# Scores of the forgetting attention: two heads on two row tiles, split operands, and a new order of the second block

## The reference, cut to what matters

```
log_f = log_sigmoid(fl + b_forget)            # (L, 12)
F = cumsum(log_f)                             # forget sums, one row of 512 per head
s = (q * 64**-0.5) @ k.T + F[t] - F[s]        # causal: s <= t, else -1e30
p = softmax(s);  o = p @ v
y_fox = o * silu(gf)
```

## Time and profile before

| | |
|---|---|
| median of 3 runs | 1972.76 us (1971.41 to 1973.77) |
| span of the profiled execution | 1970.0 us |
| PE busy | 1925.6 us (98%) |
| DVE, ACT, POOL busy | 1198.0, 923.5, 945.3 us |
| chain that ended last, share of PE | 89% |

### The profile page before, as it was taken

One profiled execution on the slowest core, in us unless ns is written; L12 is line 12 of the kernel. 1 busy time (PEld: TensorE's weight loads), 2 busy tenths in 40 slices (PEclk: granted clock), 3 DMA queues, 4 the chain that ended last, 5 costly groups with the idle time before them and its releaser, 6 DMA issues.

```text
span 1970.0 us, 28999 instructions
## 1 busy us (share of the span) xinstructions
PE 1925.6 (98%) x11395; PEld 1595.0 (81%) x11395; DVE 1198.0 (61%) x1932; ACT 923.5 (47%) x1747; POOL 945.3 (48%) x702
## 2 busy tenths in 40 slices
PE   6999999999999999999999999999999999999998
PEld 5878787888788878888888888888688777889986
DVE  6587979694566646664544440345765575876664
ACT  4555756564455544233434342344655454534442
POOL 1343323234534226564444444454474561788883
PEclk9999999999999999999999999999999999999999
DMA  8256353543321117664332334335122323233333
GB/s 310 76 168 191 110 182 117 182 145 105 107 62 55 43 56 285 226 227 158 96 107 86 107 85 148 99 115 187 55 74 81 82 55 115 85 98 97 89 121 138
DMA packets 92327, 242.48 MB, mean 123 GB/s; under 512 B 28192, under 2 KB 31392, under 8 KB 90784
## 3 DMA queue, kind: packets, MB, share of 16 engines
q1 hardware_dynamic: 89312, 232.24, 37.3%
q10 hardware_dynamic: 2880, 8.39, 1.1%
HBM read 223.14 MB, written 14.29 MB: 121 GB/s over the span
## 4 chain that ended last, share of the span: by engine, by line
PE 89%; DVE 3%; POOL 3%; ACT 2%; DMA 1%; issue 1%; SPq 0%; ACTq 0%; DVEq 0%
PE ps L1002 21%; PE ps L1003 20%; PE ps L1013 20%; PE ps L1372 3%; PE ps L1447 2%; PE ps L1434 2%; PE ps L1038 1%; PE ps L1037 1%; PE ps L1422 1%; PE ps L1349 1%; PE ps L1048 1%; PE ps L1509 1%; PE ps L1103 1%; PE ps L1110 1%; PE ps L1104 1%; POOL wlo L3069 1%
## 5 line engine op out<-in xcount | busy, mean ns | idle before, releaser
L3068 POOL TENSOR_TENSOR wlo<-raww,whi 128x512 fp32r<-128x512 f32 x217 | 303.6, 1399 | 668.3 <-ACT whi L1576 667.8
L1576 ACT CAST whi<-raww 128x1024 fp32r<-128x1024 f32 (+2 forms) x299 | 295.4, 995 | 197.3 <-PE ps L1013 134.4
L3069 POOL TENSOR_TENSOR wlo<-raww,whi 128x512 fp32r<-128x512 f32 x217 | 309.7, 1427 | 0.0
L1002 PE MATMUL ps<-hT_h,whi 128*128 128x512 f32 (+1 forms) x688 | 251.3, 374 | 2.4 <-DVE st L2480 1.7
L1003 PE MATMUL ps<-hT_l,whi 128*128 128x512 f32 (+1 forms) x688 | 244.6, 365 | 0.0
L1013 PE MATMUL ps<-hT_h,wlo 128*128 128x512 f32 (+1 forms) x688 | 152.4, 364 | 0.0
L1002 PEld LDWEIGHTS ps<-hT_h,whi 128*128 128x128 f32 x688 | 129.8, 189 | 27.3 <-issue 3.4
L1003 PEld LDWEIGHTS ps<-hT_l,whi 128*128 128x128 f32 x688 | 129.9, 189 | 21.9 <-issue 1.7
L1013 PEld LDWEIGHTS ps<-hT_h,wlo 128*128 128x128 f32 x688 | 119.2, 189 | 20.7 <-issue 0.5
L1002 PE MATMUL ps<-h_h,whi 128*128 128x512 f32 x336 | 130.7, 389 | 0.0
L1003 PE MATMUL ps<-h_l,whi 128*128 128x512 f32 x336 | 130.7, 389 | 0.0
(11 more groups left out here) (642 smaller groups left out, 4863.8 us busy)
## 6 DMA issues: line engine op xcount, KB each, us to landing
ec<-csd SPq DMA_DIRECT2D x32, 1024.0 KB, 8.2
raww<-in_w_up SPq DMA_DIRECT2D x44, 512.0 KB, 3.6
modr<-in_w_mod SPq DMA_DIRECT2D x32, 512.0 KB, 5.9
raww<-in_w_xbc SPq DMA_DIRECT2D x24, 512.0 KB, 3.8
raww<-in_w_gl SPq DMA_DIRECT2D x24, 512.0 KB, 3.9
raww<-in_w_z SPq DMA_DIRECT2D x16, 512.0 KB, 3.6
raww<-in_w_g SPq DMA_DIRECT2D x16, 512.0 KB, 3.6
raww<-in_w_os SPq DMA_DIRECT2D x16, 512.0 KB, 4.0
```

Of the source, the lines that this page charges most:

```text
L1002: e.matmul(o, whi[:, i, c], hi(k)[:, t0:t1], start=(k == 0), stop=False)
L1576: e.copy(o, x.rearrange("p (k c) -> p k c", c=64) if p == plan.first["dt", 0] else x).then_inc(*w_high.mark(("high", p)))
L3068: e.tensor_tensor(o[:, 0:512], x[:, 0:512], h[:, 0:512].bitcast(F32), ALU.subtract).then_inc(*p_wlow.mark(("first half", p)))
L3069: e.tensor_tensor(o[:, 512:1024], x[:, 512:1024], h[:, 512:1024].bitcast(F32), ALU.subtract).then_inc(*p_wlow.mark(("split", p), ("raw fre ...
```

## The change: what it does

1. q and k of two heads stay together, head 2p in rows 0 to 63 and head 2p+1 in rows 64 to 127, as a high part (ACT, one instruction of 128 rows) and a low part (DVE, one scalar_tensor_tensor out of PSUM) in the tiles fhead0 and fhead1. The bank of `fq` is marked "out of" by the DVE instruction, no longer by ACT.
2. The step `fscore` is now for a pair p and a group g of query rows: g 0 is rows 0 and 1, g 1 row 2, g 2 row 3. For each row it issues three fp32r products (high by high, low by high, high by low), head by head in turn on rows 0 to 63 and 64 to 127 of the array and into two banks; then one fp32r product that picks the head's row of forget sums; then two bf16 products for the mask (128 and 64 columns).
3. The forget sums are split in a high and a low row set in the tile frows by DVE, which also builds the pick matrix, two identities and two masks in bf16. FT, its 12 DMAs and the clearing of qk on POOL are gone; POOL clears eyes and frows.
4. DVE and ACT do softmax work for both heads of a pair within one step.
5. The order of the second block is one written list, `second_block_steps()`. Eight `fpt` of a pair are grouped (`turns(p)`), and `fqout 0` stands behind `s5bar 1`.

```diff
+def second_block_steps():
...
+    o = [("fq", 0), ("s5zero",)] + [("s5u", m) for m in range(3)]
+    o += [("s5bar", 0), ("fq", 6), ("s5bar", 1), ("fqout", 0), ("fqout", 6)]
+    o += [tm(0, 0)] + pw(0, 1) + [tmout(0, 0), tm(0, 1)] + pw(1, 3) + [tmout(0, 1), tm(0, 2)] + pw(3, 4)
+    o += [tmout(0, 2), tm(0, 3)] + pw(4, 6) + [tmout(0, 3), ("fq", 1)] + pw(6, 8) + [("fqout", 1)]
+    o += [("fscore", 0, 0)] + pw(8, 9) + [("fscore", 0, 1)] + pw(9, 10) + [("fscore", 0, 2)] + pw(10, 11)
+    o += [("fq", 7), ("fscored", 0)] + pw(11, 13) + [("fqout", 7)] + pw(13, 15) + [("fq", 2)] + pw(15, 17) + [("fqout", 2)]
+    o += turns(0)[:4] + pw(17, 18) + turns(0)[4:] + pw(18, 19)
+    o += [("fscore", 1, 0)] + pw(19, 20) + [("fscore", 1, 1)] + pw(20, 21) + [("fscore", 1, 2)] + pw(21, 23)
+    o += [("fq", 8), ("fscored", 1)] + pw(23, 25) + [("fqout", 8), ("fpv", 0)] + pw(25, 26) + [("gf", 0), ("fout", 0)] + pw(26, 28)
+    o += [("gfout", 0)] + pw(28, 29) + turns(1) + pw(29, N_POW) + s5(0, "tab", "q")
+    o += [("fscore", 2, 0), ("fscore", 2, 1), ("fscore", 2, 2), ("fq", 3), ("fscored", 2), ("fqout", 3)] + s5(0, "g")
...
+    o += [("fscore", 3, 0), ("fscore", 3, 1), ("fscore", 3, 2)] + s5(0, "out") + [("fq", 4)] + s5(0, "gelu") + [("fscored", 3)]
+    o += s5(0, "tanh") + [("fqout", 4)] + s5(0, "y") + s5(1, "q") + [("fpv", 2)] + s5(1, "k") + [("s5u", 3)] + s5(1, "x")
...
-                    for i, a in {0: ((0, 0), (1, 128)), 1: (), 2: ((2, 0),), 3: ((3, 0),)}[n]:
-                        Wd = (i + 1) * 128
-                        e.matmul(ps[:, b, a:a + Wd], fqk(h, 0)[:, i * 128:(i + 1) * 128], fqk(h, 1)[:, 0:Wd], start=True, stop=False)
-                        e.matmul(ps[:, b, a + i * 128:a + Wd], maskb[:, 0, :], maskb[:, 2, :], start=False, stop=True).then_inc(
-                            *scores_done.mark(("fscores", h, i)))
+                    for n in FGROUP[g]:
+                        a, Wd, c = (128 if n == 1 else 0), (n + 1) * 128, slice(n * 128, (n + 1) * 128)
+                        for q, kk in ((fhigh, fhigh), (flow, fhigh), (fhigh, flow)):
+                            for h, b in zip(pair, banks):
+                                e.matmul(ps[:, b, a:a + Wd], q(p, 0)[fside(h), c], kk(p, 1)[fside(h), 0:Wd],
+                                         start=(q is fhigh and kk is fhigh), stop=False)
+                        for h, b in zip(pair, banks):
+                            e.matmul(ps[:, b, a:a + Wd], pickf[fside(h), h:h + 1].to_broadcast([64, P]), frows[fside(h), 0:Wd], start=False, stop=False)
+                        for half, w in ((0, 128), (1, 64)):
+                            for h, b in zip(pair, banks):
+                                last = e.matmul(ps[:, b, a + Wd - w:a + Wd], eyes[fside(h), 64 - 64 * half:192 - 64 * half],
+                                                fmask[fside(h), 128 * half:128 * half + w], start=False, stop=(half == 1))
...
+                    e.tensor_tensor_scan(fu, ones[0:12, 0:1].to_broadcast([12, L]), fl, 0.0, ALU.mult, ALU.add).then_inc(*v_step.mark())
+                    e.tensor_tensor(fold[:, :], ident[:, 0:32], ident[:, 32:64], ALU.add).then_inc(*v_step.mark())
...
+                    e.tensor_copy(frows[0:12, :], fu).then_inc(*v_step.mark())
+                    e.tensor_tensor(fold[:, :], fold[:, :], ident[:, 64:96], ALU.add).then_inc(*v_step.mark())
+                    e.tensor_copy(frows[64:76, :], frows[0:12, :].bitcast(F32)).then_inc(*v_step.mark())
+                    e.tensor_tensor(frows[32:44, :], fu, frows[0:12, :].bitcast(F32), ALU.subtract).then_inc(*v_step.mark())
+                    e.tensor_copy(frows[96:108, :], frows[32:44, :].bitcast(F32)).then_inc(*v_step.mark())
+                    e.tensor_tensor(pickf[:, :], fold[:, :], ident[:, 96:128], ALU.add).then_inc(*v_step.mark())
+                    for r in (slice(0, 64), slice(64, 128)):
+                        e.tensor_copy(eyes[r, 64:128], ident[r, r]).then_inc(*v_step.mark())
+                        e.tensor_copy(fmask[r, 0:128], maskb[0:64, 2, :]).then_inc(*v_step.mark())
+                        e.tensor_copy(fmask[r, 128:192], maskb[64:128, 2, 64:128]).then_inc(
...
+                elif k == "fqout":
...
+                    e.scalar_tensor_tensor(out=flow(p, i), in0=ps[:, bank_of((src, 0)), :], scalar=1.0 if i else 0.125,
+                                           in1=fhigh(p, i).bitcast(F32), op0=ALU.mult, op1=ALU.subtract).then_inc(
+                        *v_xlow.mark(("out of", (src, 0)), ("fq", m)))
```

More of the change, by code:

```diff
@@ L688, in program @@
         y5_out = [signal(f"y5_out{i}", by=16) for i in range(2)]
-        f_row = [signal(f"f_row{i}", by=16) for i in range(4)]
         swap_in = [signal(f"swap_in{i}", by=16) for i in range(2)]
@@ L1496, in tensor_program @@
                 elif k == "fscore":
-                    _, h, n = s
-                    if h == 0 and n == 0:
+                    _, p, g = s
+                    pair = (2 * p, 2 * p + 1)
+                    if p == 0 and g == 0:
                         ring_of_gemms[0] = OLDEST
-                    if n != 1:
-                        b = bank(s, OLDEST)
-                        PE.wait_ge(at("fq", h // 2))
-                        PE.wait_ge(at("fq", 6 + h // 2))
-                        PE.wait_ge(at("forget row", h))
-                        PE.wait_ge(at("rows of ones"))
@@ L1507, in tensor_program @@
-                    for i, a in {0: ((0, 0), (1, 128)), 1: (), 2: ((2, 0),), 3: ((3, 0),)}[n]:
-                        Wd = (i + 1) * 128
-                        e.matmul(ps[:, b, a:a + Wd], fqk(h, 0)[:, i * 128:(i + 1) * 128], fqk(h, 1)[:, 0:Wd], start=True, stop=False)
-                        e.matmul(ps[:, b, a + i * 128:a + Wd], maskb[:, 0, :], maskb[:, 2, :], start=False, stop=True).then_inc(
-                            *scores_done.mark(("fscores", h, i)))
+                    banks = [bank(("fscore", h, FGROUP[g][0]), OLDEST) for h in pair]
@@ new lines, in tensor_program @@
+                    PE.wait_ge(at("fq", p))
+                    PE.wait_ge(at("fq", 6 + p))
+                    PE.wait_ge(at("forget rows"))
+                    for n in FGROUP[g]:
[10 more added lines that the diff above has]
+                                                fmask[fside(h), 128 * half:128 * half + w], start=False, stop=(half == 1))
+                                if half:
+                                    last.then_inc(*scores_done.mark(("fscores", h, n)))
@@ L3384, in sync_program @@
                             *y5_out[m % 2].mark(*[("y5 stored", m)] * (t == 7)))
-                elif k in ("forget", "fqout"):
-                    m = s[1] if k == "fqout" else 0
-                    if k == "forget":
-                        SP.wait_ge(at("forget sums"))
-                        SP.wait_ge(at("rows of ones"))
-                    if k == "forget" or 0 < m < 6:
-                        for h in (2 * m, 2 * m + 1):
-                            if h >= 4:
-                                SP.wait_ge(at("fscores", h - 4, 3))
-                            e.dma_start(fqk(h, 1)[64:65, :], FT[h:h + 1, :]).then_inc(*f_row[h % 4].mark(("forget row", h)))
                 elif k == "yin":
```

181 lines of the change are left out of this document (72 added, 109 removed), and 4 rows, old and new, of the table AHEAD_OF.

## The result

The changed kernel takes 1997.0 us (median of 4 runs, 1995.3 to 1998.7) against 1972.9 us before (1971.4 to 1973.8): a ratio of 1.0125, interval 1.011 to 1.0139. It is slower by 24 us where 2.5 us less were forecast, and outside the range. The profiled execution took 1995.3 us with a span of 1994.0, against a span of 1970.0 before.

What follows compares the result with a forecast made beforehand. PE's queue, 89% of the chain of waits, was taken to set the end. The terms -9.1 + 5.2 + 3.7 - 3.3 + 1.0 = -2.5 us took 1972.8 to 1970.3 us, range 1961.5 to 1980.

Steps and rivals of the forecast that it cites:

- Part 1: Score products on PE: a pair takes 3.7 us instead of 2.61 a head, -9.1 us (bounds -13.9 and +8.3).
- Part 3: Bank of `fq 0`: PE stands before the first value chunk until DVE empties it, +5.2 us (4.3 to 6.8).
- Part 4: Pairs 0 and 1 on DVE: its backlog makes PE stand at pair 2's scores, +3.7 us (0 to 6).
- The old waits: PE's two waits of 1.9 and 1.3 us among the last `s5pow` steps go, -3.3 us.
- Part 5: At `s5k 1`: PE waits for POOL's `s5q`, with too little work between in group 1, +1.0 us.
- Rival D: After PE's first stand the clock halves (+2.9) and low parts make pair 3 late: together +5, 1975.5 us; chance 0.16.
- Rival C: Score products: row tiles do not run side by side, 1975.5 us, or 1984 if products queue too; chance 0.16.
- B: Rival: a pair costs about 3.2 us, ACT and DVE keep up, no backlog: -8.9, 1963.9 us; chance 0.26.

Runs made afterwards that it cites:

- head by head: The changed kernel with all score products of one head issued before the other's, instead of product by product in turn: 1996.9 us.
- pow ahead: The changed kernel with steps 8 to 15 of `s5pow` moved ahead of the first scores: 1995.8 us.
- Extra matmuls: The changed kernel with matmuls that nothing reads ahead of four PE waits: 1999.1 us; repeated with two of the placements one group earlier: 1996.3 us.
- the three together: The changed kernel with low parts first, pow ahead, and `s5q 1` and `s5q 3` directly behind `s5out 0` and `s5out 2`: 1987.7 us.
- low parts first: The changed kernel with `fqout 0` and `fqout 6` ahead of the S5 constants in the list: 1992.4 us.

## Why the prediction was wrong

**Part 1** had the right mechanism, and 3.7 us a pair were 3.33 (-11.3 in place of -9.1, masks and changes of shape being cheaper than priced). What it left out is that the gain holds only while PE sets the end; head by head shows that here it doesn't.

**Part 3** is the first step that failed, by size. The mechanism was right and seen at once: PE stands at the first value chunk, released by the new low part. The term "3.9 us" for DVE's preparation of the forget rows measured 7.8: 1353.77 to 1361.54. Four of the small instructions took 1.16 to 1.47 us where 0.2 to 0.45 was priced:

```profile
1353.96 1.47 DVE L2818 CAST frows<-ffs 12x512 fp32r<-12x512 f32 x1
1355.36 1.26 DVE L2819 TENSOR_TENSOR fold<-fold,cst 128x32 f32<-128x32 f32 x1
...
1358.69 1.16 DVE L2829 COPY fmask<-maskb 64x64 bf16<-64x64 bf16 x1
1359.88 1.23 DVE L2827 CAST eyes<-cst 64x64 bf16<-64x64 f32 x1
```

The prediction had seen such stretches beside POOL's weight splits and assumed "as often as before". All four began while POOL was at a weight split (1353.86 to 1356.58 and 1358.46 to 1361.06), and each of the last three ended within 0.06 us of a split's end. More instructions in a stretch where POOL works meet more of them. The constants behind were 1 us shorter, so the wait was 7.7 us and not 5.2. Its upper end of 6.8 was too low too.

**A second gap of part 3** is in its last sentence: "against the first scores DVE has 8 steps of pow and two low parts to do while PE does 17 us; no second wait there". There was none, indeed, but DVE then idled 12.7 us with the rest of pow queued behind a low part. Filling it by itself (pow ahead) gave 1.2 us.

**Part 4** priced a backlog as DVE's sum of work against PE's and put it at pair 2's scores, +3.7. The sum of work was right (its terms add to 39.4, not to the 39.0 it wrote, which changes little): from pair 0's first score at 1389.19 to pair 2's at 1435.63 DVE was busy 39.0 us. The 45 us from the first scores on, as in the earlier trace rows:

```profile
1389.00:1434.00 45.00, 39.45 (x250) 30.91 (x248) 37.46 (x126) 27.53 (x67) 18.23 (x16) 0.92 0.21 69
```

That is 37.5 of 45 where the earlier trace rows had 34.7, and the stage took 46.4 us, so DVE was idle for 7.4 of them. Yet PE waited 7.2 us for it: 2.9 for the bank of `fq 2`, 2.5 for that of the gate, 1.8 for turned columns. The step that failed is to price a wait by the difference of the two sums. An in-order engine is late for one result because of what is queued ahead of that result, not because of its total. The old waits went, as forecast (-3.3).

**Part 5** priced POOL's `Qc` at `s5k 1`, +1.0, measured 1.24 once nothing lay over it. That the same step also has DVE copies, behind `fqout 4`, which waits for ACT, behind two others, was missed: 4.9, and 3.2 at `s5k 3`. Part 5 looked at one of `s5q`'s two engines.

**The clock.** Rival D had it: +2.9 forecast for the first chunk, 1.7 measured. It was thought of for one stand. There were four, and pairs 1 and 2, the very products the change made cheap, lost 5.5 us to it. The Trainium skill, "TensorE: Matmul & The Clock Gate", on oscillation, is borne out now, by 0.50 behind four stands, though not behind every one. Extra matmuls show that taking it away at three places alone gives back less than 1 us of the median, so it is a part of PE's account more than a cause of the time.

**The sum.** Forecast -9.1 + 5.2 + 3.7 - 3.3 + 1.0 = -2.5. Measured in the same terms: -11.3 + 7.7 + 7.2 - 3.3 + 8.1, that is +8.4; with 3.0 of other new waits (22.7 in sum), 7.2 of half clock at pairs 1 and 2 and the first chunk, the 3.4 that remain in the account above, and 2.1 upstream it is 24. Rival C was wrong in its mechanism, B in its claim that DVE keeps up. No rival held all of it.

## What to carry to other kernels

Price a new order engine by engine: for every result that the bound engine waits for, list what stands ahead of it in its producer's queue, the second producer of a step included. Sums of busy time tell little of this: DVE's were as forecast, and PE waited for it all the same. And a cheaper product on the bound engine is worth its time only if that engine doesn't stand behind it; run the old products in the new order (and, which was not done here, the new products in the old one) before believing either.

## What the hardware showed

- Products on 64 rows of two heads in turn: 3.33 us a pair, 4.01 head by head. Even head by head is less than the 5.2 us (8 x 0.646, part 1) that the same products would take at the whole array's distances, without the masks. There PE started products of one half ahead of products of the other half that were queued before them.
- DVE's instructions of 128x24 take 0.2 us alone. Of 175 that, in the twenty traces between 1320 and 1750 us, began under a POOL instruction that still had 0.2 us or more to run, 170 took 0.65 to 1.36 us, and each ended 0.03 to 0.07 us behind that POOL instruction; of 1200 that met none, all took less than 0.3. A squaring step took 1.3 and 5.3 us.
- The granted clock fell to 0.50 behind waits of 7.7, 4.9, 2.9, and 2.5 with 1.8 us, and partly (0.76) behind one of 1.4 in the three together; behind another of 1.4, at the first chunk with low parts first, it stayed at 1.00. Behind the 3.2 us ahead of `s5k 3` it stayed at 1.00 in the changed kernel and read 0.66 from 1588 to 1592 with low parts first. So the length of a wait alone doesn't tell.
